# Hybrid decoder step on one core: weighing the samples' cached values ahead of the attention, and turning keys, gate columns and samples' rows between its heads

## What is computed

```python
h = rms_norm(x); aq, ak, av, mqk, mv, mg, mo = split(h @ w_in)
q, k = rope(head_rms_norm(aq)), rope(head_rms_norm(ak))
# attention, 8 heads of 64: three dilated windows (128,1), (512,4), (2048,16), merged by softmax weights
# mLSTM, 8 heads of 64: decays from the gates, chunked scan, head norm, output gate
x = x + concat(attention, mlstm) @ w_out
x = x + peer(rms_norm(x))    # product-key retrieval over 16384 single-neuron experts
```

## Time and profile before

| | us |
|---|---|
| Three timed runs | 1863.43, 1877.28, 1883.02 |
| Their median | 1877.28 |
| The profiled execution, its own time | 1858.25 |
| Its span in the trace | 1856.2 |
| Mean granted clock of TensorE | 0.985 |
| PE busy, share of the span | 1801.8 (97%) |
| DVE busy | 1217.6 (66%) |
| ACT busy | 572.3 (31%) |
| POOL busy | 491.5 (26%) |

### The profile page before, as it was taken

How to read it: one execution, slowest core, us unless ns; L and a number is a source line. 1 busy time by engine, 2 the same in 40 slices (tenths; PEclk the granted TensorE clock), 3 DMA queues, 4 the chain that set the end, 5 groups by cost and what they waited for, 6 DMA issues and landing times.

```text
span 1856.2 us, 31074 instructions
## 1 busy us (share of the span) xinstructions
PE 1801.8 (97%) x12753; PEld 1329.0 (72%) x12753; DVE 1217.6 (66%) x2611; ACT 572.3 (31%) x984; POOL 491.5 (26%) x515
## 2 busy tenths in 40 slices
PE   8999988989999999999999999999989999999999
PEld 6743445668888888888888888888855666665665
DVE  7558658364899993656655424334349787979794
ACT  1002133320233323334444333343323333323231
POOL 0001100000165670000000000000077877776740
PEclk9999989798999999999999999999999999999999
DMA  4422622002113234455555565445399999999991
GB/s 166 107 87 109 200 78 106 1 4 114 46 47 121 85 140 164 174 208 189 222 228 228 194 244 194 172 171 194 125 396 377 364 382 377 377 368 382 356 373 64
DMA packets 116813, 368.26 MB, mean 198 GB/s; under 512 B 12104, under 2 KB 72760, under 8 KB 104896
## 3 DMA queue, kind: packets, MB, share of 16 engines
q1 hardware_dynamic: 90992, 291.17, 41.8%
q0 software_dynamic: 25680, 75.10, 11.2%
HBM read 301.35 MB, written 64.88 MB: 197 GB/s over the span
## 4 chain that ended last, share of the span: by engine, by line
PE 82%; DVE 11%; DMA 3%; issue 2%; ACT 1%; SPq 1%; DVEq 0%; ACTq 0%
PE psum L1995 34%; PE psum L2046 22%; PE psum L1702 22%; PE psum L2016 2%; DMA a_in<-d_act 2%; DVE u_lo L1442 1%; DMA v_raw<-in_v 1%; DVE v_lo L1599 1%; SPq L525 1%; PE psum L1708 1%; PE psum L1830 0%; DVE rest L1369 0%; PE psum L1750 0%; PE psum L1793 0%; DMA xT<-in_xT 0%
## 5 line engine op out<-in xcount | busy, mean ns | idle before, releaser
L2046 PE MATMUL psum<-w_hl,v_hi 128*128 128x384 bf16 x2048 | 501.0, 327 | 8.3 <-DVE w_hl L1632 8.3
L1995 PE MATMUL psum<-h_hi,u_hi 128*128 128x260 bf16 x2048 | 394.5, 274 | 3.4 <-DVE u_lo L1442 2.6
L1995 PE MATMUL psum<-h_lo,u_hi 128*128 128x260 bf16 x2048 | 394.2, 274 | 0.0
L1995 PE MATMUL psum<-h_hi,u_lo 128*128 128x260 bf16 x2048 | 394.1, 274 | 0.0
L696 POOL DMA_INDIRECT trow<-in_v,t_lists x136 | 172.7, 1270 | 658.4 <-ACT act_f L903 588.1
L2046 PE MATMUL psum<-w_hl,v_lo 128*128 128x384 bf16 x1024 | 334.8, 327 | 0.0
L2046 PEld LDWEIGHTS psum<-w_hl,v_hi 128*128 128x128 bf16 x2048 | 200.7, 98 | 141.6 <-DVE v_lo L1599 9.3
L1442 DVE TENSOR_TENSOR u_lo<-u_raw,u_hi 128x1024 bf16<-128x1024 f32 x128 | 153.9, 1216 | 209.1 <-ACT u_hi L891 209.1
L903 ACT ACTIVATE act_f<-psum 128x520 f32<-128x520 f32 x128 | 77.3, 604 | 468.0 <-PE psum L1995 468.0
L1995 PEld LDWEIGHTS psum<-h_lo,u_hi 128*128 128x128 bf16 x2048 | 198.4, 97 | 31.1
L1995 PEld LDWEIGHTS psum<-h_hi,u_lo 128*128 128x128 bf16 x2048 | 198.4, 97 | 30.9
(11 more groups left out here) (373 smaller groups left out, 1831.0 us busy)
## 6 DMA issues: line engine op xcount, KB each, us to landing
u_raw<-in_uT SPq DMA_DIRECT2D x32, 2048.0 KB, 9.5
v_raw<-in_v SPq DMA_DIRECT2D x32, 2048.0 KB, 14.6
wr<-in_w SPq DMA_DIRECT2D x13, 2048.0 KB, 7.7
d_gate<-stage SPq DMA_DIRECT2D x12, 2048.0 KB, 8.0
d_act<-act_f SPq DMA_DIRECT2D x20, 768.0 KB, 4.3
g_in<-d_gate SPq DMA_DIRECT2D x10, 1536.0 KB, 24.2
a_in<-d_act SPq DMA_DIRECT2D x20, 768.0 KB, 16.1
g_up<-d_gate SPq DMA_DIRECT2D x12, 768.0 KB, 9.3
```

The source lines that it names most:

```text
L1995: mm = pe.matmul(upair[n % 2][:, f, 0:HALF], w[g % 2][:, k, c * P:(c + 1) * P], hs[:, k, halves[f]], start=(k == 0 and x == 0), stop=(k == ...
L2046: mm = pe.matmul(ybank[m][:, 0:DENSE], w[g % 2][:, c, m * P:(m + 1) * P], w_hl[g % 2][:, z, c, :], start=(g == 0 and c == 0 and x == 0), s ...
```

## The change

Three things move; no arithmetic changes.

1. DVE weighs samples 0 to 3 between the state's last step (`Cs`) and the wait for its stores. In the heads only samples 4 to 7 are weighed, at the same head-steps as before.
2. The six banks "kt" 0 to 3, "aT" and "mA" are made inside the heads, on PE behind the PT product of head-steps 9, 13, 17, 21, 25 and 29, on ACT between the exps of head-steps 10 and 11, 14 and 15, and so on. In the ring they stand in the same places (`TURNED`). The loops behind the heads are gone.
3. On ACT, `decay(1)` comes before `keys_decayed(0)`, and no copy stands between them.

```diff
+TURNED = {8: ("kt", 0), 12: ("kt", 1), 16: ("kt", 2), 20: ("kt", 3), 24: ("aT",), 28: ("mA",)}
 def psum_plan():
...
         u += [("S", *at) for at in att[n + 2:n + 4]] + [("PT", *at) for at in att[n:n + 2]]
-    u += [("aT",)] + [("kt", i) for i in range(NPT)]
+        if n in TURNED:
+            u += [TURNED[n]]
     pair = lambda h: [("ST", h + x, k) for k in range(3) for x in range(2)]
     u += [("nM", 0), ("nM", 1)] + pair(0)
-    u += [("mA",)]
# ACT
                 if h == 3 and i >= 1:
                     attended(i - 1)
+                if n - 2 in TURNED:
+                    key = TURNED[n - 2]
+                    bk = arrived(act, key)
+                    if key[0] == "kt":
+                        if key[1] == 0:
+                            act.wait_ge(kp_out, KP_OUT)
+                        copy(key, ktok[:, key[1], :], bk[:, :])
+                    elif key[0] == "aT":
+                        copy(key, st[:, 48:112], bk[:, 0:64])
+                    else:
+                        copy(key, mixA[:, :, SEQ:NT], bk[:, 0:4 * DB].rearrange("p (c t) -> p c t", c=4))
             attended(NPT - 1)
-            bk = arrived(act, ("aT",))
-            copy(("aT",), st[:, 48:112], bk[:, 0:64])
-            act.wait_ge(kp_out, KP_OUT)
-            for i in range(NPT):
-                bk = arrived(act, ("kt", i))
-                copy(("kt", i), ktok[:, i, :], bk[:, :])
...
             decay(0)
+            decay(1)
             keys_decayed(0)
-            decay(1)
-            bk = arrived(act, ("mA",))
-            copy(("mA",), mixA[:, :, SEQ:NT], bk[:, 0:4 * DB].rearrange("p (c t) -> p c t", c=4))
# DVE, behind the step on Cs
+            def weigh_values(b):
+                values = cache_arrived(v, DB + b)[:, :, :].rearrange("p g (h d) -> p g h d", h=H)
+                probs = PTs[:, :].rearrange("p (g b h) -> p g b h", g=3, b=DB)[:, :, b, :]
+                tt(values, values, probs.unsqueeze(3).to_broadcast([P, 3, H, DH]), ALU.mult).then_inc(v_weighted, 1)
+
+            for b in range(4):
+                weigh_values(b)
             v.wait_ge(ms_out, MS_OUT)
...
             inverse_sum(0)
-            weigh_values(0)
             inverse_diagonal(0)
...
-                if n % 3 == 0 and n // 3 + 1 < DB:
+                if n % 3 == 0 and 4 <= n // 3 + 1 < DB:
                     weigh_values(n // 3 + 1)
# PE
+            def turned(key):
+                bk = claim(pe, key)
+                if key[0] == "kt":
+                    for c in range(4):
+                        mm = turn(bk[:, c * P:(c + 1) * P], qkT[:, 4 + c, key[1] * P:(key[1] + 1) * P], P)
+                elif key[0] == "aT":
+                    pe.wait_ge(enm_done, 1)
+                    for x, src in enumerate((arow, enm)):
+                        for i in range(NPT):
+                            mm = turn(bk[:, x * 32 + i * H:x * 32 + (i + 1) * H], src[:, i * P:(i + 1) * P], H)
+                else:
+                    pe.wait_ge(new_done, 2)
+                    for c in range(4):
+                        mm = turn(bk[:, c * DB:(c + 1) * DB], dtok[:, c * P:(c + 1) * P], DB)
+                made(mm, key)
...
                 if n % 2 == 0 and n >= 2:
                     values(n - 2)
+                if n - 1 in TURNED:
+                    turned(TURNED[n - 1])
             values(len(ATT) - 2)
...
```

More of the change, by code:

```diff
@@ L1190, in inverse_diagonal @@
                 ts(inv_sum[n % 4][:, :], ident, st[:, 36 + n % 4:37 + n % 4], None, ALU.mult).then_inc(att_inv, 1)
-            def weigh_values(b):
-                values = cache_arrived(v, DB + b)[:, :, :].rearrange("p g (h d) -> p g h d", h=H)
-                probs = PTs[:, :].rearrange("p (g b h) -> p g b h", g=3, b=DB)[:, :, b, :]
-                tt(values, values, probs.unsqueeze(3).to_broadcast([P, 3, H, DH]), ALU.mult).then_inc(v_weighted, 1)
             row_max(0)
@@ L1846, in _ @@
                     values(n - 2)
+                if n - 1 in TURNED:
+                    turned(TURNED[n - 1])
             values(len(ATT) - 2)
-            pe.wait_ge(enm_done, 1)
-            bk = claim(pe, ("aT",))
-            for n, src in enumerate((arow, enm)):
-                for i in range(NPT):
-                    mm = turn(bk[:, n * 32 + i * H:n * 32 + (i + 1) * H], src[:, i * P:(i + 1) * P], H)
-            made(mm, ("aT",))
-            for i in range(NPT):
-                bk = claim(pe, ("kt", i))
-                for c in range(4):
-                    mm = turn(bk[:, c * P:(c + 1) * P], qkT[:, 4 + c, i * P:(i + 1) * P], P)
-                made(mm, ("kt", i))
             def minus_max(h):
@@ L1888, in _ @@
             decay_scores(0)
-            pe.wait_ge(new_done, 2)
-            bk = claim(pe, ("mA",))
-            for c in range(4):
-                mm = turn(bk[:, c * DB:(c + 1) * DB], dtok[:, c * P:(c + 1) * P], DB)
-            made(mm, ("mA",))
             def numerators(h):
```

## The result

| | before | after |
|---|---|---|
| Timed runs, median (lowest to highest) | 1870.02 us (1858.82 to 1884.54), 19 runs | 1858.19 us (1851.18 to 1865.34), 19 runs |
| Profiled span, clock | 1856.2 us, 0.985 | 1859.5 us, 0.985 |

The ratio is 0.994 with a 95% interval of 0.9922 to 0.9958: 11.2 us faster, between 8 and 15. Two later measurements of the same changed kernel gave 0.9927 (0.9903 to 0.9951) and 0.9931 (0.9907 to 0.9956), and the kernel before measured against itself 0.9992 (0.9969 to 1.0016). So the gain is real, although the profiled execution of the changed kernel was 3.3 us *longer* than the one of before. Both things have to be explained.

What follows compares the result with a forecast made beforehand. The prediction took PE to bound most of the chain (82%), at half clock in the first heads, with DVE pacing heads 5 to 15. 5.8 - 1.1 - 0.9 + 4.3 = 8.1 us gain, forecast 1866 us, range 1850 to 1879.

Steps and rivals of the forecast that it cites:

- The cover of the weighings: Behind `Cs`, DVE idles 10.73 us; the four moved weighings take 7.0 us of it, leaving 3.7 us.
- The clock of the first heads: Heads 0 to 4: PE's clock stays at 2.4 GHz; with the moved weighings worth 5.8 us, ends 2.7 and 6.9.
- some 8 us: First heads: how much sooner after the first scores the PT product of head 5 should come at full clock.
- the first rival: The clock stays low in the first heads: 2.7 us instead of 5.8, gain 5.0, time 1869 us; chance 22%.
- The turns in the heads: Transposes of six banks moved inside the heads: cost 1.1 us on PE, plus 0.9 us for ACT's copies.
- the ring: Bank claims in the heads: no term needed, each waits for a bank freed at least a head-step before.
- the 0.9 us put in for the copies: Heads: loss from ACT's six copies between exps, 0.9 us, with ends of 0 and 6.6.
- The rival of the copies: Heads: copies hold up ACT's exps, costing 6.6 us instead of 0.9; gain 2.4, time 1872 us; chance 10%.
- Behind the heads: After the last head: 24 turns go, decay(1) comes earlier, samples' turns go; gain 4.3 us, ends 3.3 and 4.8.
- a better clock behind the heads: Rival: the clock recovers behind the heads too, worth some 6 us; gain 14, time 1860 us; chance 12%.
- wrong in kind: Signs: DVE waits ahead of its weighings, or the heads' gain is given back at the first DMA-bound wait further on.
- The slower case: Rival: the clock falls once more inside heads 16 to 31; 4 us slower, 1878 us; chance 8%.

Runs made afterwards that it cites:

- a1: The changed kernel once more, unaltered, for a second profile and more timed runs; ratio to before 0.9927 (0.9903 to 0.9951).
- e1: The kernel before with only the four weighings moved ahead of the wait for the stores; ratio to before 0.9958 (0.9927 to 0.9990).
- e3: The kernel before with only ACT's decay(1) put ahead of keys_decayed(0); ratio to before 0.9961 (0.9928 to 0.9993).
- b1: The kernel before once more, unaltered, measured against itself, for a second profile; ratio 0.9992 (0.9969 to 1.0016).
- a2: The changed kernel once more, unaltered, for a third profile; ratio to before 0.9931 (0.9907 to 0.9956).
- e2: The changed kernel with the weighings put back in the heads, leaving the turns and ACT's order; ratio to before 0.9946 (0.9914 to 0.9978).
- e5: The kernel before with three more PE products in the empty stretch behind the last head; ratio to before 0.9952 (0.9929 to 0.9975).

## Why the prediction was right

The forecast said 8.1 us of gain and 1866 us, in a range from 1850 to 1879; measured were 11.2 us and 1858.2. Direction, size and range hold, but the likeliest value was 8 us too high. Its parts fared differently. The means over the three profiles of each kernel, up to the last up product, give the account:

| | forecast | before | changed | measured |
|---|---|---|---|---|
| First scores to last `values` | 5.8 - 1.1 - 0.9 = 3.8 | 69.0 | 65.9 | 3.0 (5.1 at full clock, -1.0 at half) |
| To the first output product | 4.3 | 13.2 | 8.8 | 4.5 |
| To the first `head_out` | 0 | 12.3 | 10.0 | 2.3 |
| To the last up product | 0 | 988.0 | 986.1 | 1.9 |
| Sum | 8.1 | | | 11.7 |

The sum stands so near to the timed 11.2 us partly by luck. Outside the table the changed kernel's first scores come 1.1 us earlier in the mean and its tail is 4.0 us longer, and the mean spans of the three and three profiles lie 8.8 us apart.

**The cover of the weighings** was as stated: no wait ahead of them, 3.99 us left of it (2.9 to 4.0 in the other profiles with them moved) for a forecast of 3.7.

**The clock of the first heads** was the step that the forecast took as given and that is a matter of the execution. At full clock the heads gain 5.1 us net, and with the 1.5 us of the turns added back the weighings and the clock are worth 6.6, against 5.8 forecast, near the upper end of 6.9. Head 5 comes 5.8 us sooner (13.5 to 7.7 us after the first scores); the "some 8 us" that the prediction looks for there do not follow from its own terms, 1.65 + 3.7. Its sum for PE's work from head 0 to head 5 was too large, 6.1 us for a measured 5.6 (a1, 258.90 to 264.48): the durations of the rows overlap, one PT product and the next starting 0.42 us apart though each is listed with 0.49. At half clock the first profile had no gain at all but a loss of 1.0 us, where the first rival gave the heads a gain of 0.7. That rival was mis-sized. It took the half clock to last as long as before, and it lasted from 257 to 272 us (13.7 us in all) in place of 258 to 269; and at half clock PE was the bound throughout, so that the fourth weighing's 1.6 us did not come back either. It came up in one of three.

**The turns in the heads**: 1.5 us measured for 1.1 + 0.9 = 2.0, but made up of other parts. From the PT product of head 16 to the last `values` the changed kernel needs 35.2 us and e1, without turns, 34.1: **1.1 us**. The chain shows the four key transposes at 0.44, twice (forecast 0.41), and the samples' at 0.34 (0.3), 1.2 together. The gate columns' 0.58 at 309.07 are on the chain and yet cost nothing, since `dtok` keeps PE waiting soon after; 0.97 us of wait are left there, 1.56 before, so all of it was hidden as said:

```profile
313.80 1.13 PE L1709 MATMUL psum<-inv_sum,Pb 128*128 128x128 f32 x8 [0.97 <-DVE inv_sum L1204]
```

The other 0.45 us are lost in heads 8 to 15 (17.1 us from the PT product of head 8 to that of head 16, 16.7 in e1), where the forecast put turns, and the ring, at nothing. It is the ring. A turned bank shifts the places behind it, so that behind the bank of head 13 the scores of head 17 need the bank of head 15's scores, which DVE's `row_max` has not read yet. PE waits for it in every profile of the changed kernel and in none of before (a1):

```profile
280.94 0.91 PE L1709 MATMUL psum<-kT,qT 64*128 64x384 f32 x2 [0.64 <-DVE stats L1193]
```

"Each claim behind a turned bank waits for a bank that DVE or ACT freed at least a head-step before" does not hold there. For ACT's queue the list of waits in heads 16 to 31 (us in total, times, longest) has a line which the kernel before does not have there:

```profile
DVE stats L1198 <- ACT Pb L802: 2.6, 3, 1.0
```

DVE's reciprocal waits for an exp three times, a microsecond at the longest. That is the copy in front of the exp, the effect that the Trainium skill's "strict FIFO" (TensorE: Matmul & The Clock Gate, architectural detail) speaks of. It is there, at 2.6 us of DVE's time. But these heads got no longer than by the turns' own work (1.1 us for 1.2), so nothing of it shows on the path: the 0.9 us put in for the copies were not lost, still less the 6.6. The rival of the copies falls.

**Behind the heads** the step held best: 4.5 us for 4.3, in each of the three profiles, of which 1.08 are the decays' order (e3, forecast 1.06). The rest is the 24 turns and the samples' rows.

**The clock further on** is where the forecast was too small. It gave 12% to a better clock behind the heads, worth 6 us. In the means it is worth 4.2 (2.3 + 1.9), and it came in all three profiles of the changed kernel and in one of three of before. The reason given for it was wrong. The empty stretch that got shorter is not needed: e1 and e3 have the good clock with that stretch unchanged or nearly so. The kernel before simply meets the fall in a worse place in two of three executions, where PE has 9 to 12 us of full work in the mLSTM's first numerators. Changes of one or several microseconds ahead of it seem to move that.

That the kernel before lies at half clock longer than its variants is seen over all timed executions, and not only in the few profiles. The mean of their granted clocks was 0.9812 in the kernel before and 0.9844 in e3 on one chip; 0.9827 before and 0.9868 changed (a1) on a second; and 0.9833 before, 0.9835 in b1 and 0.9884 changed (a2) on a third, with standard errors of 0.0002 to 0.0007. A difference of 0.001 in this mean, over 1860 us, is 3.7 us more or less at half clock, and worth up to 1.9 us where PE is the bound. By this estimate the clock is worth at most 8 to 9.5 us in the changed kernel and 6 in e3. The mean covers the whole span, the tail too, so it does not say where. It can account for e3's 7 us for 1 us of work. It also means that the parts do not add: e1's 0.42% and e2's 0.54% make 0.96, the two together gave 0.60 to 0.73, as they would if both had won much the same half clock back; with these intervals it is not shown. What in the edits moves the clock stays open. In e5 the profile does not show where the gain lies: its landmarks gain 1.7 us over the mean of before and its timed runs 9, but its timed executions have 0.9857 for 0.9827, worth up to 5.6 us.

**Why the first profile was longer nevertheless**: up to the last up product it leads by 10.2 us (1329.3 for 1339.5) and loses 13.5 in the tail. There the kernel streams values and weights from memory. The tail of before's first profile was 516.7 us, which neither of its repetitions reaches (528.5, 534.1), and the changed kernel has 530.0 to 531.2. The difference arises at the start of the tail, where the DMA share is 1.00 and more in at least one of the windows and PE waits at its first products with the streamed weights (the trace lists most of this as "issue", so it does not name what is late). These are the windows of before and of the changed kernel:

```profile
1345.00:1370.00 25.00, 25.00 (x155) 15.07 (x154) 4.47 (x6) 4.87 (x7) 19.52 (x19) 1.00 1.03 397
1370.00:1400.00 30.00, 23.15 (x128) 13.01 (x126) 23.01 (x30) 11.27 (x15) 18.41 (x16) 0.89 1.00 378
```

```profile
1345.00:1370.00 25.00, 14.53 (x63) 6.40 (x61) 12.48 (x17) 5.94 (x8) 19.82 (x18) 0.73 1.05 398
1370.00:1400.00 30.00, 25.16 (x137) 13.50 (x136) 14.19 (x17) 6.13 (x9) 10.09 (x11) 0.94 0.51 197
```

In the whole tail PE waited 8.3 us before and 15.8 changed, and from 1345 to 1400 it had 6.8 and 17.1 us at half clock. That is 7.5 us and at most 5.1, together 12.6 of the 13.5 us. The repetitions of before look like the changed kernel: 14.6 and 17.2 us of waits, 20.5 and 27.3 us at half clock. Why that one execution waited less is not shown.

So the tail differs by 17 us between executions of the same kernel, more than the whole change is worth, and a comparison of single spans would have had the wrong sign. It also leaves open whether the changed kernel gives a part of its gain back at this wait, which the prediction named as a sign of being wrong in kind: the mean tails, 530.5 and 526.4 us, differ by less than those of one kernel do. That the timed gain is not smaller than the forecast one speaks against it.

**Why 1866 was too high**: the forecast's 1866 + 8.1 is a base of 1874, between the median of three runs (1877.3) and the mean of these with the fast profiled execution (1870.5). 19 runs put it at 1870.0, and the gain was 3 to 4 us larger than forecast.

**The slower case** did not come: heads 16 to 31 kept the clock at 1.00 in all three profiles of the changed kernel.

## What to carry to other kernels

Ask of every piece of work that is to be moved whether its engine is the bound in that very stretch *and at that clock*: the same four weighings, with the clock that came along, were worth 6.6 us in two executions, and half a microsecond in a third in which PE ran at half clock. Compare two versions by landmarks inside the trace, and take more than one profile of each, before reading a difference of spans: one profile here had the wrong sign. And a change that wins more in the timed runs than its landmarks explain may only have moved the place of a clock fall, so test it with an edit that is known to be worth almost nothing (e3), and with the kernel against itself.

## What the runs showed of the hardware

The granted clock fell to 0.50 in stretches where PE was busy throughout (from 346 to 358 us in b1 at a mean of 0.57 with 12.00 of 12.00 us busy, and PE had been busy 7.00 of 7.00 us from 340 to 347), and in others it stayed at 1.00 with PE busy 1.38 of 3.7 us (a1, 254.7 to 258.4). So PE's busy share in the profile does not tell by itself when the clock falls. Nor does a gap by itself: behind the same two gaps of 1.42 and 1.40 us it fell in one profile of the changed kernel and stayed in two. The falls come back in the same places in two executions of the same kernel within a microsecond (b1 and the first profile of before: 258, 329, 346, 418 and 602 us), and a third execution whose heads began 5 us later had them elsewhere.
